# Constant matmuls on an idle TensorE at the boundaries of a six-part encoder step

## The reference

```python
h = _sub_in(x, mod, i, g_pre)            # rmsnorm(x) * (1 + scale) + shift
x = x + res_w * (1 + gate) * rmsnorm(out, g_post)
```

## Time and profile before

| | us |
|---|---|
| median of 3 runs | 2628.42 (2628.07 to 2632.04) |
| profiled execution: device time | 2632.73 |
| profiled execution: span, first to last instruction | 2630.9 |
| PE busy in the span | 2425.5 (92%) |
| DVE, ACT, POOL busy in the span | 1552.9, 856.0, 338.3 |
| mean granted clock of TensorE | 0.957 |

### The profile page before, as it was taken

The page is one execution under the profiler, slowest core; times in us unless marked ns, Lnnn a source line. Parts: engine busy times, 40 slices in busy tenths (PEclk is TensorE's granted clock), DMA queues, the critical chain, the costliest instruction groups (busy, mean ns, idle before and its releaser), DMA issues. The chain is left out here.

```text
span 2630.9 us, 44404 instructions
## 1 busy us (share of the span) xinstructions
PE 2425.5 (92%) x18216; PEld 2316.4 (88%) x18216; DVE 1552.9 (59%) x2767; ACT 856.0 (33%) x1764; POOL 338.3 (13%) x426
## 2 busy tenths in 40 slices
PE   7999999889997799999979999986999886999997
PEld 6999999878885699999969999985888786999997
DVE  3377768655556756667574665756555557443323
ACT  2222222344544332222232222233444443222222
POOL 0000002421011500001230000233011133000002
PEclk9999999889997899999989999997999988999999
DMA  6255545322222124454413554532233221342331
GB/s 222 66 161 168 169 135 162 97 60 68 69 66 69 36 86 141 137 152 141 133 49 105 152 148 130 149 96 67 73 92 91 73 59 49 110 121 84 87 87 62
DMA packets 392697, 277.59 MB, mean 106 GB/s; under 512 B 11104, under 2 KB 349824, under 8 KB 392496
## 3 DMA queue, kind: packets, MB, share of 16 engines
q1 hardware_dynamic: 385792, 254.77, 32.9%
q0 software_dynamic: 6704, 19.99, 2.6%
HBM read 263.48 MB, written 12.81 MB: 105 GB/s over the span
## 5 line engine op out<-in xcount | busy, mean ns | idle before, releaser
L894 PE MATMUL lin<-h_hi,w_hi 128*128 128x272 f32 x2720 | 600.2, 293 | 36.6 <-DVE h_lo L1784 36.4
L894 PE MATMUL lin<-h_hi,w_lo 128*128 128x272 f32 x2720 | 592.4, 291 | 0.0
L894 PE MATMUL lin<-h_lo,w_hi 128*128 128x272 f32 x2720 | 590.9, 290 | 0.0
L1629 DVE TENSOR_TENSOR w_lo<-raw,w_hi 128x1024 fp32r<-128x1024 f32 (+1 forms) x270 | 329.3, 1224 | 290.3 <-ACT w_hi L1266 289.4
L894 PEld LDWEIGHTS lin<-h_hi,w_hi 128*128 128x128 f32 x2720 | 442.2, 190 | 44.9 <-DVE h_lo L1784 28.8
L894 PEld LDWEIGHTS lin<-h_lo,w_hi 128*128 128x128 f32 x2720 | 443.4, 191 | 0.3
L894 PEld LDWEIGHTS lin<-h_hi,w_lo 128*128 128x128 f32 x2720 | 440.6, 191 | 0.0
L1266 ACT ACTIVATE w_hi<-raw 128x1024 fp32r<-128x1024 f32 (+1 forms) x270 | 276.3, 1032 | 181.9 <-DMA raw<-in_ffn_w_down 151.0
L1668 DVE SCALAR_TENSOR_TENSOR acc<-raw,silu_c,acc 128x512 f32<-128x512 f32 x448 | 313.1, 758 | 0.0
L894 PE MATMUL lin<-act_hi,w_hi 128*128 128x272 f32 x1296 | 286.4, 292 | 6.6 <-DVE w_lo L1629 6.4
L894 PE MATMUL lin<-act_hi,w_lo 128*128 128x272 f32 x1296 | 283.4, 289 | 0.0
(11 more groups left out here) (260 smaller groups left out, 3542.3 us busy)
## 6 DMA issues: line engine op xcount, KB each, us to landing
raw<-in_w_ada SPq DMA_DIRECT2D x128, 512.0 KB, 3.8
raw<-in_ffn_w_gate SPq DMA_DIRECT2D x88, 512.0 KB, 3.8
raw<-in_ffn_w_up SPq DMA_DIRECT2D x88, 512.0 KB, 3.8
raw<-in_ffn_w_down SPq DMA_DIRECT2D x64, 448.0 KB, 4.1
raw<-in_ffn_w_down SPq DMA_DIRECT2D x32, 512.0 KB, 4.7
raw<-in_w_in_ab SPq DMA_DIRECT2D x24, 512.0 KB, 3.8
raw<-in_w_in_c SPq DMA_DIRECT2D x24, 512.0 KB, 3.9
start_w<-in_w_ada SPq DMA_DIRECT2D x16, 512.0 KB, 12.4
```

The costliest lines, as they stand in the source:

```text
L894: m = nc.tensor.matmul(out[a], w[:, k, :], mv[:, k0 + k, half(a)], start=first and k == 0 and n == 0, stop=last and k == u["tiles"] - 1 an ...
L1629: nc.vector.tensor_tensor(w_l[:, 0:u["tiles"], :], raw[:, u["slot"], 0:u["tiles"], 0:w_l.shape[-1]], w_h[:, 0:u["tiles"], :].bitcast(F32), ...
```

## The change

A function `fill(n, bank)` issues `n` float32 matmuls of the constant `ident` (128x128) with 128 columns of the constant `mean_w` into a bank of PSUM that nobody reads at that time. It is called

- in the gradual units of `head` for `j > 0`: 8 fills before the first block's wait, 4 before each of the seven others, in both halves;
- before the units `u1`, `g2`, `u2` of half 0 of an ffn head for `j > 0`: 6, 4 and 4, after the unit's wait for its banks and before that for its weights;
- at the end of each of the steps 0 to 13 of a mixer's last stage: 3;
- before the wait for each of the four differential heads: 4;
- after the last `mean`: 8.

That is 360 + 42 + 84 + 16 + 8 = 510 fills. Also, PE now waits at the start of a head for the coefficients of all jobs of the sub-layers before (`job_coef`), since the fills of the heads write to `ps_o`.

```diff
+IDLE_FIRST = (8, 4)
+IDLE_SLOT = (6, 4, 4)
+IDLE_END = 8
+IDLE_STEP = 3
+IDLE_NORM = 4
...
+            def fill(n, bank=ps_o):
+
+                for _ in range(n):
+                    nc.tensor.matmul(bank[:, 0:P], ident[:], mean_w[:], start=True, stop=True)
+
+            def jobs_before(j):
+                return len(START) + sum(len(q[i]) for q in (GU_JOBS, DN_JOBS) for i in q if i < j)
+
-            def chunk(name, halves, out, hi, lo, k0=0, first=True, last=True, gradual=None, mid=None):
+            def chunk(name, halves, out, hi, lo, k0=0, first=True, last=True, gradual=None, mid=None, idle=(0, 0)):
...
+                if gradual is None:
+                    fill(idle[0])
                 if ws.count[name, halves[0]] == min(ws.count[name, 0], ws.count[name, 1]):
                     pe.wait_ge(lo_done, u["idx"] + 1)
...
                     if gradual is not None:
+                        fill(idle[0] if k == 0 else idle[1])
                         pe.wait_ge(h_lo_done, gradual + k + 1)
...
                 prev = j - 1
+                if j > 0:
+                    pe.wait_ge(job_coef, jobs_before(j))
                 for a in (0, 1):
                     for i, name in enumerate(names):
                         mid = None
+                        idle = (0, 0)
+                        if j > 0 and i == 0:
+                            idle = IDLE_FIRST
+                        elif j > 0 and kind == "ffn" and a == 0 and i >= 3:
+                            idle = (IDLE_SLOT[i - 3], 0)
...
                     if s < 10 and s % 2 == 0:
                         scores(s)
                         scores(s + 1)
+                    if st.st == 8 and s < STEPS:
+                        fill(IDLE_STEP, lin[:, 1, :])
...
                         for hd in range(4):
+                            fill(IDLE_NORM, lin[:, 1, :])
                             pe.wait_ge(b_scaled, hd + 1)
...
             mean(NSUB - 1, 1)
+            fill(IDLE_END)
```

More of the change, by code:

```diff
@@ L978, in head @@
                             out = {a: lin[0:16, b, 0:HALF] if k is None else bank(b)}
-                        chunk(name, (a,), out, h_hi, h_lo, gradual=2 * KT * j + KT * a if i == 0 else None, mid=mid)
+                        chunk(name, (a,), out, h_hi, h_lo, gradual=2 * KT * j + KT * a if i == 0 else None, mid=mid, idle=idle)
             def gate_up(j):
```

## The result

| | before | after |
|---|---|---|
| median of 5 runs | 2630.1 us (2628.07 to 2633.3) | 2643.64 us (2641.15 to 2645.72) |
| profiled execution, span | 2630.9 | 2639.4 |
| PE busy, mean granted clock | 2425.5, 0.957 | 2495.1, 0.987 |

The changed kernel takes 1.005 of the time of the one before, with a 95% interval of 1.0035 to 1.0065: 13.5 us slower, outside the 0.2% within which two versions can't be told apart. Forecast were 2638, in a range of 2626 to 2648, with 0.69 for slower.

A forecast was written before the change was run, and what follows sets the result against it. PE, busy 92% of the span, sets the pace except in stretches where it waits; there fills are free, elsewhere they add. 17.3 + 1.3 + 1.5 - 5.2 - 5.2 = +9.7 on 2628.4: about 2638 us, range 2626 to 2648.

The forecast's parts named there:

- half 1 of ffn heads: Fills before the blocks of `g0`, where PE goes at full pace, delay dense work: 7.9 us per head, +23.3 in all.
- half 0 of ffn heads: Fills fit in waits for weights; `mean` and `u2` gain from full clock in j = 2 and 3: -5.95 us.
- ab head: Half 1 of mixer ab's head: fills make PE set the pace, partly repaid by faster matmuls behind: +1.3 us.
- c head: Half 1 of mixer c's head: as in ab, after a 9 us wait, and not absorbed later: +1.5 us.
- ab end: Mixer ab's last stage, differential heads' norm and `o` gain 1.8, 0.9 and 2.5 us from full clock: -5.2.
- c end: Mixer c's last stage and output projection run faster at full clock: -5.2 us.
- half-clock rival: Clock still falls where fills precede long waits, above all before `u2` and mixers' half 1: +10, 2648 us; chance 0.14.
- cover rival: Fills before `g0` in half 1 of ffn heads lie in waits for `h_lo`; three quarters hidden gives 2620 us; chance 0.10.
- -1.45 for the `mean` in j = 2: Half 0 of that ffn head: `mean`, at half clock for 3.1 us, takes 1.6 at full clock, gaining 1.45.
- transposes' rival: Transposes don't raise the clock, so the norm's heads pay 0.4 each and `o` stays at half: +5, 2643 us; chance 0.05.
- The balance: The mixers' ends bring the 16 us of their bound: 2632 us, not distinguishable from no change; chance 0.13.

The follow-up runs named there:

- The last version: Changed kernel without fills in first units or after the last mean, and with 8 before the first differential head: 2616.65 us against 2630.06 for the kernel before, ratio 0.9953.
- the run with half 1 alone: Kernel before plus only the 72 fills in half 1 of the mixers' ab and c heads: 2633.74 us against 2630.06, ratio 1.0015.
- the second trace of the changed kernel: Profiled execution of the changed kernel run once more, unchanged: median 2642.68 us against 2632.14 for the kernel before, ratio 1.0039.
- steps-only run: Kernel before plus only the 84 fills in the mixers' last stages, 3 per step: 2621.02 us, ratio 0.9966 to the kernel before.

## Why the prediction held, and where its terms were off

One trace of before was the yardstick of every term, and the runs showed how far a single one misleads. So the table's stages are averaged here over all the traces that have all the fills of a stage and over all that have none there, the one of before among these as 0. The difference is the better price. The last version, which has only the slots in half 0, stands on neither side there. Three to ten traces stand on a side.

| term | forecast | with | without | price |
|---|---|---|---|---|
| half 1 of ffn heads, j = 2, 3, 5 | +23.3 | 8.0, 7.7, 7.2 | 0.5, -0.2, -0.2 | 22.9 |
| half 0 of ffn heads, j = 2, 3, 5 | -5.95 | -2.5, -2.3, -0.2 | -1.9, -0.8, 1.3 | -3.6 |
| ab head | +1.3 | 2.6 | 0.3 | 2.4 |
| c head | +1.5 | 0.8 | -0.7 | 1.4 |
| ab end | -5.2 | -4.1 | -0.4 | -3.7 |
| c end | -5.2 | -5.1 | 0.9 | -6.0 |
| sum | +9.7 | | | +13.4 |

The sum lies by the medians, +13.5 and +10.5, where the forecast's was +9.7; that it meets the first of them so closely is chance, since the traces behind most prices differ by 1 us and more among themselves. The forecast's own errors are +1.5 for the ab end, +1.1 for the ab head and +2.35 for half 0, and smaller ones the other way. The median of 2643.64 alone would not tell the forecast (2638) from the half-clock rival (2648), to which it is nearer; the terms do. The bounds that the prediction gives for the mixers' heads and ends add up to 2629 to 2646, not to the 2631 to 2644 that it states.

**Half 1 of the ffn heads** was right, in place, mechanism and price: 7.9 forecast each, 7.4 to 7.9 measured, no gap between fills and blocks. The experiments with and without these fills (+22.2 alone, 19 to 20 of the change) show it, and refute the cover rival: of 23.8 us for 108 fills 22.9 were paid, so some 4 of them were hidden, where it needed 44 to break even.

**Half 0 of the ffn heads** is the step that failed: of the 5.95 us only some 3.6 are real by the traces and 3.2 by the medians, which also hold the mixers' half 0. The prediction took what one execution did at half clock for what the kernel does. The -1.45 for the `mean` in j = 2 is the clearest case: it runs at full clock in every other trace. In the six others without fills in that head the stage is 1.1 to 3.0 us shorter than in the trace of before; `u2` is at full clock in three of them and partly at half in three. Fills don't hold it up each time either: in half 0 with the ends its 24 matmuls take 4.7 us where they take 3.2 at full clock. In j = 5 it went the other way. I booked 0 since the trace showed full clock, and without fills other executions lose up to 3.5 there, which in five of five traces with fills does not happen.

**The mixers' heads**: together 2.8 forecast, 3.8 by the table, 3.7 (1.6 to 6.3) by the run with half 1 alone. In the ab head the term was mis-sized, 1.3 for 2.4. Blocks and pay-back together came out at 1.1; nearly two blocks were at half clock (530.35 to 534.50 in the changed kernel), where one and a half were counted. What the term lacks is the second fall of the clock at 551 us, which costs 1.5. A fill at half clock was priced at 0.45 us and takes 0.39 (1.56 / 4). For c the run with half 1 alone shows 0.1 in its trace, and the traces without fills spread from -2.4 to 0.3, so its 1.4 is the least certain of the prices. In two of the three traces with all fills of the mixers' heads a further 1.5 us lies late in ab's stages. It is a fall of the clock, too, which the other traces don't have there; in the second trace of the changed kernel, and then in the first:

```profile
753.60:756.90 3.30, 3.30 (x14) 3.02 (x16) 0.22 (x1) 0.40 (x2) 3.30 (x6) 0.50 0.61 175
...
753.60:756.90 3.30, 2.21 (x17) 1.72 (x18) 0.76 (x3) 1.60 (x9) 1.33 (x3) 1.00 0.53 159
```

**The ends** came out at 9.7 of 10.4. The clock was forecast over 0.9 in the last stages: 0.95 and 1.00. In the changed kernel the 5.2 of the ab end are, by the pairs, 1.3 in the stage (1.8 forecast), 1.3 in the four heads of the norm (0.9) and 2.5 in `o` (2.5). The heads were forecast to come every 2.1 us. They came after 2.26, 2.80 and 2.20 us (819.38, 821.64, 824.44, 826.64), against 2.7 before; the 2.80 is the head at which the clock is down once more (820.7 to 824.0). With fills beside the norm only, the heads gained just 0.1 and `o` 2.5. On average less is gained in ab, since in four of the seven traces with fills in both parts the clock fell a second time, in `o`, which then took 4.6 us in place of 3.1. In the second trace of the changed kernel:

```profile
828.70:832.00 3.30, 3.30 (x16) 3.30 (x15) 2.21 (x2) 0.76 (x1) 0.00 (x0) 0.50 0.19 52
```

The steps-only run gave 9.0 where I had expected 6.5 of it, but its interval, 5.5 to 12.6, holds both.

**The transposes' rival** fell. In the experiment the granted clock was 0.92 and 1.00 with transposes and the time the same. The Trainium skill, "TensorE: Matmul & The Clock Gate", Part 4: PE-mode transpose, holds that full clock does not engage for transposes; in this kernel they raise it and keep it, as the earlier trace rows had suggested.

**The half-clock rival** is half right in ab (the clock falls again about the start of its half 1 and, at times, in its end) and wrong elsewhere: the ffn heads are at 0.94 to 0.97. **The balance** needed 16 us from the ends; they give some 10. The last 8 fills cost nothing that can be told from the spread: from j = 5 to PE's last transpose the traces with them are 0.2 to 0.3 us longer than the one before, those without -0.4 to 0.3. The wait for coefficients stands in every version, those that beat the kernel before too; by itself it wasn't tried.

## What to carry to other kernels

Constant matmuls pay where TensorE both waits often and lies on the chain, here the last stages of the mixers: 100 of the 510 fills brought nearly all of the gain that could be shown; the 222 of half 0 brought 3.2 us by themselves and nothing measurable beside these. A loop that passes twice, once for each half, must be looked at twice: the same call was covered in half 0 and bare in half 1, and 0.22 us each on the path ate the gain twice over. And where the granted clock decides, price a stage from several executions; one trace told 5.95 us where 3.6 were to be had.

## What was not expected of the hardware

**Where the clock falls isn't fixed.** In stages with waits the same instructions took up to 3.5 us more or less from one execution to the next, though nothing in them had changed. Fills ahead of a long wait don't help behind it: in the ab head 8 of them lie before half 1, and the first block is at half clock still.

**A busy TensorE can stay at half clock.** In the changed kernel's second trace, near the start, PE multiplies with two moving columns. The stretch, and the timeline of PE in it:

```profile
60.00:84.00 24.00, 24.00 (x112) 24.00 (x113) 4.16 (x12) 2.40 (x5) 0.00 (x0) 0.50 0.08 24
```

```profile
59.74 6.33 PE L928 MATMUL ps_o<-silu_c,start_w 128*128 128x2 f32 x29
65.93 13.79 PE L928 MATMUL ps_t<-silu_c,start_w 128*128 128x2 f32 x64
79.58 0.57 PE L910 MATMUL lin<-h_hi,w_hi 128*128 128x272 f32 x1
```

PE is busy for all of the 24 us, the 93 records of this shape take 20 of them, and the clock is 0.50 throughout, on into the first projection matmuls. Nor did matmuls of this shape keep the clock where it was up. In the same trace it was 1.00 while `x` was transposed, and fell while PE did 64 of them without a pause:

```profile
30.00:36.70 6.70, 5.92 (x47) 5.12 (x47) 6.60 (x15) 3.99 (x6) 0.00 (x0) 1.00 1.07 372
36.80:43.90 7.10, 7.10 (x35) 7.10 (x35) 0.35 (x2) 2.94 (x4) 0.00 (x0) 0.50 0.90 244
```

In the other traces the clock's column reads 1.00 for this part of the program, but the projection matmuls behind it start every 0.23 us there too (from 83.74 on in the changed kernel's first trace), which is the pace of half clock; so the column can't be trusted there. A row of PE that is busy does not by itself tell that the clock is up; the clock has to be read beside it.
